# Feed-forward's first product by Strassen's seven sub-products, with nine hidden tiles kept in DRAM

## The reference

```python
def dwconv(x, w):   # three taps along the rows, per column
...
def conv_ffn(h, p):
    u = dwconv(h @ p['w_up'], p['ffn_conv']) + p['ffn_conv_b']
    val, gate = jnp.split(u, 2, axis=-1)
    return (val * jax.nn.silu(gate)) @ p['w_down']
...
        x = x + gt1 * rmsnorm(y, p['g_post_mix'])
        h = modulate(rmsnorm(x, p['g_pre_ffn']), sh2, sc2)
        x = x + gt2 * rmsnorm(conv_ffn(h, p), p['g_post_ffn'])
```

## Time and profile before

| | us |
|---|---|
| three runs: lowest, median, highest | 3891.1, 3891.55, 3891.93 |
| the profiled execution, its own time | 3886.74 |
| its span, first to last instruction | 3885.0 |
| PE busy in the span | 3590.0 (92%) |
| DVE busy, ACT busy | 1754.6 (45%), 962.5 (25%) |
| mean granted TensorE clock | 0.962 of full |

### The profile page before, as it was taken

How to read it: one execution, slowest core, us unless ns; L and a number is a source line. 1 busy time by engine, 2 the same in 40 slices (tenths; PEclk the granted TensorE clock), 3 DMA queues, 4 the chain that set the end, 5 groups by cost and what they waited for, 6 DMA issues and landing times.

```text
span 3885.0 us, 63673 instructions
## 1 busy us (share of the span) xinstructions
PE 3590.0 (92%) x28989; PEld 2243.8 (58%) x28989; DVE 1754.6 (45%) x2533; ACT 962.5 (25%) x1900; POOL 47.3 (1%) x114
## 2 busy tenths in 40 slices
PE   7998879989999996789999998999899799999988
PEld 3546655559988986344444443444566444777753
DVE  2048852245556555332222220022999663544524
ACT  3015620135455553121111110000011301233320
POOL 2000000000000000000000000000000000000000
PEclk9999989989999998899999999999999899999999
...
GB/s 221 22 43 66 66 65 7 28 6 17 4 17 4 4 4 5 114 103 36 30 44 44 43 22 38 44 54 103 22 33 33 43 60 67 22 27 28 1 76 65
DMA packets 108143, 168.08 MB, mean 43 GB/s; under 512 B 5203, under 2 KB 66386, under 8 KB 107234
## 3 DMA queue, kind: packets, MB, share of 16 engines
...
## 4 chain that ended last, share of the span: by engine, by line
PE 84%; DVE 9%; ACT 4%; DMA 2%; issue 1%; SPq 0%; ACTq 0%; DVEq 0%
PE psum_all L66 83%; ACT sbuf_all L75 3%; DVE sbuf_all L102 3%; DVE sbuf_all L94 3%; DVE sbuf_all L84 2%; PE psum_all L69 1%; ACT L75 1%; DMA sbuf_all<-in_w_mod 1%; DMA sbuf_all<-in_w_out 1%; DVE sbuf_all L91 0%; DVE sbuf_all L108 0%; DMA sbuf_all<-in_gla_w_out 0%; DVE sbuf_all L90 0%; DMA sbuf_all<-in_w_up 0%; DMA sbuf_all<-in_w_down 0%
## 5 line engine op out<-in xcount | busy, mean ns | idle before, releaser
...
L75 ACT ACTIVATE sbuf_all<-psum_all 128x512 f32<-128x512 f32 (+7 forms) x969 | 434.6, 468 | 1569.0 <-PE psum_all L66 1441.7
L94 DVE SCALAR_TENSOR_TENSOR sbuf_all<-sbuf_all 128x1040 f32<-128x1040 f32 (+8 forms) x571 | 624.0, 1094 | 24.8 <-PE psum_all L66 4.5
L75 ACT ACTIVATE sbuf_all<-sbuf_all 128x64 f32<-128x64 f32 (+12 forms) x449 | 259.9, 589 | 952.8 <-DVE sbuf_all L78 394.8
L84 DVE TENSOR_TENSOR sbuf_all<-sbuf_all 128x640 f32<-128x640 f32 (+10 forms) x497 | 403.9, 833 | 187.0 <-ACT sbuf_all L75 147.7
L78 DVE COPY sbuf_all<-psum_all 128x256 f32<-128x256 f32 (+5 forms) x137 | 71.1, 526 | 540.5 <-PE psum_all L66 526.4
L91 DVE TENSOR_SCALAR sbuf_all<-sbuf_all 128x1024 f32<-128x1024 f32 (+9 forms) x131 | 76.5, 589 | 470.3 <-ACT sbuf_all L75 467.7
L75 ACT ACTIVATE sbuf_all<-psum_all,sbuf_all 128x1280 f32<-128x1280 f32 (+5 forms) x212 | 164.3, 781 | 351.4 <-PE psum_all L66 323.2
L108 DVE COPY_PREDICATED sbuf_all<-sbuf_all,psum_all 128x256 f32<-128x256 int32 (+2 forms) x296 | 145.5, 493 | 159.3 <-PE psum_all L66 154.5
L69 PE MATMUL psum_all<-sbuf_all 128*128 128x128 f32 (+2 forms) x771 | 115.0, 294 | 56.2 <-DVE sbuf_all L90 27.0
L90 DVE TENSOR_SCALAR sbuf_all<-sbuf_all 128x256 f32<-128x256 f32 (+9 forms) x149 | 57.5, 424 | 209.1 <-ACT sbuf_all L75 206.3
L69 PEld LDWEIGHTS psum_all<-sbuf_all 128*128 128x128 f32 (+2 forms) x771 | 92.9, 152 | 91.8 <-DVE sbuf_all L90 30.1
...
...
## 6 DMA issues: line engine op xcount, KB each, us to landing
sbuf_all<-in_w_mod SPq DMA_DIRECT2D x12, 2048.0 KB, 8.2
...
sbuf_all<-in_w_in SPq DMA_DIRECT2D x6, 2048.0 KB, 7.8
...
sbuf_all<-in_w_down SPq DMA_DIRECT2D x4, 2048.0 KB, 7.6
...
sbuf_all<-in_x ACTq DMA_DIRECT2D x2, 2048.0 KB, 19.9
```

The source lines that it names most:

```text
L75: return self.e.activation(out, in_, func, bias=bias, scale=scale, **kw)
L84: return self.e.tensor_tensor(out, a, b, op) if self.e is not None else Unissued()
L94: return self.e.scalar_tensor_tensor(out, a, s, b, op0, op1) if self.e is not None else Unissued()
```

## The change

`up` takes `h` and each pair of weight tiles as 2 x 2 blocks: the 1024 columns of `h` in two halves of four tiles ("low", "high"), the 1024 rows in two halves of 512, and a value tile and a gate tile as the two outputs. One level of Strassen's scheme (in Winograd's form) makes the four output blocks of a pair from seven products of half the depth, in place of eight. So a pair is 7 x 4 = 28 matmuls where it was 32. The operands are sums and differences: of `h`'s blocks, made once for the stage by VectorE (`row_sums`, four operations of 128x2048, three into new places, one over `rows12`), and of the weights' blocks, made for each pair (`weight_sums`, four operations of 128x512, one of them over the block `w21` in its slot). The outputs are put together from four banks a to d: banks a, c and d take two products each, the second added to the first, with a copy of a (by ScalarE) or an addition out of c or d (by VectorE) between the two. There are five such additions of 128x512 on VectorE per pair, and two bank copies on ScalarE in place of four. The convolution and the multiplication of pair p come while TensorE works on pair p + 1.

The row sums and weight sums lie where the first nine hidden tiles were. Those nine tiles are made in a staging buffer, go out to DRAM on ScalarE's queue (512 KB each), and come back in two loads (one tile, then eight) on SyncE's queue when all engines have ended `up`. `down` takes its weight blocks in another order and size: hidden tiles 15 to 21, then 8 to 14, then 0 to 7. The diff, with the removed bodies of functions that stand above left out:

```diff
-UPS = [(blk, half, gate) for blk in range(KF // 2) for half in range(2) for gate in range(2)]
+UPS = [(blk, half) for blk in range(KF // 2) for half in range(2)]
+SPILLED = 9
 def up_memory(K):
     sb = K.sb
     sb.at = K.hT_at
     K.hid = sb.take(KF * L2, k=KF)
     assert sb.at <= K.h2T_at
     sb.at = K.h2T_at + KD * SEQ
-    K.up_raws = K.slots([sb.take(SEQ + 2) for _ in range(2)])
+    K.up_raws = [sb.take(SEQ + 2) for _ in range(2)]
     K.cv, K.cg = sb.take(SEQ), sb.take(SEQ)
+    K.up_part, K.hid_stage = sb.take(512), sb.take(SEQ)
+    low, high, one, two = slice(0, 4), slice(4, 8), slice(0, 512), slice(512, SEQ)
+    K.rows11, K.rows12, K.rows21, K.rows22 = (K.h2T[:, k, t] for k in (low, high) for t in (one, two))
+    at = K.hT_at
+    K.rows_t1, K.rows_t2, K.rows_t4 = (sb.view(at + i * 2048, 2048, k=4) for i in range(3))
+    K.w_sums = [[sb.view(at + 6144 + 1536 * i + 512 * n, 512, k=4) for n in range(3)] for i in range(2)]
+    assert 6144 + 2 * 1536 <= SPILLED * L2
+    K.hid_dram = K.nc.dram_tensor("hid_spill", (P, SPILLED, SEQ), F32).ap()
+def up_weights(w, half):
+    value, gate = slice(P * half, P * half + P), slice(256 + P * half, 256 + P * half + P)
+    return w[:, 0:4, value], w[:, 4:8, value], w[:, 0:4, gate], w[:, 4:8, gate]
 def up_tensor(K, te):
     U = K.up
     for s in K.mix.ends():
         te.wait_ge(*s)
...
+    def part(bank, lhs, rhs, opens):
+        for k in range(4):
+            done = te.matmul(bank, lhs[:, k, :], rhs[:, k, :], start=opens and k == 0, stop=k == 3)
+        return done
+    for p, (blk, half) in enumerate(UPS):
+        if half == 0:
             w = open_block(K, te, ("up", blk), 512)
...
+        w11, w12, w21, w22 = up_weights(w, half)
+        s1, s2, s4 = K.w_sums[p % 2]
+        a, b, c, d = (open_bank(K, te, "up", p, x) for x in "abcd")
+        part(a, w11, K.rows11, True).then_inc(*U.t.tick("first", p))
+        te.wait_ge(*U.v.by("s2", p))
+        te.wait_ge(*U.v.by("t2"))
+        part(b, s2, K.rows_t2, True).then_inc(*U.t.tick("both", p))
+        te.wait_ge(*U.v.by("s3", p))
+        te.wait_ge(*U.v.by("t3"))
+        part(c, w21, K.rows12, True).then_inc(*U.t.tick("differences", p))
+        part(d, s1, K.rows_t1, True).then_inc(*U.t.tick("sums", p))
+        te.wait_ge(*U.s.by("first", p))
+        part(a, w12, K.rows21, False).then_inc(*U.t.tick("one_one", p))
+        te.wait_ge(*U.v.by("t4"))
+        te.wait_ge(*U.v.by("u3", p))
+        part(c, w22, K.rows_t4, False).then_inc(*U.t.tick("two_one", p))
+        te.wait_ge(*U.v.by("s4", p))
+        te.wait_ge(*U.v.by("two_two", p))
+        part(d, s4, K.rows22, False).then_inc(*U.t.tick("one_two", p))
+        if half:
             K.weights.end(("up", blk), U.t.now())
...
     for s in K.mix.ends():
         se.wait_ge(*s)
     se.wait_ge(*U.g.by("pads"))
...
+    value = K.up_raws[0]
+    def gate(p):
+        se.wait_ge(*U.v.by("conv", p, 1))
+        se.activation(K.cg, K.cg, ACT.Silu).then_inc(*U.s.tick("silu", p))
+    def spill(p):
+        if p < SPILLED:
+            se.wait_ge(*U.v.by("hid", p))
+            se.dma_start(K.hid_dram[:, p, :], K.hid_stage).then_inc(*K.dma("spill_hid").tick(p))
+    for p in range(len(UPS)):
+        se.wait_ge(*U.t.by("first", p))
+        if p:
+            se.wait_ge(*U.v.by("one_two", p - 1))
+        se.activation(K.up_part, K.bank.view("up", p, "a"), ACT.Copy).then_inc(*U.s.tick("first", p))
+        if p:
+            gate(p - 1)
+        se.wait_ge(*U.t.by("one_one", p))
+        if p:
+            se.wait_ge(*U.v.by("conv", p - 1, 0))
+        se.activation(value[:, 1:513], K.bank.view("up", p, "a"), ACT.Copy).then_inc(*U.s.tick("one_one", p))
+        K.bank.end(("up", p, "a"), U.s.now())
+        if p:
+            spill(p - 1)
+    gate(len(UPS) - 1)
 def up_vector(K, ve):
     U = K.up
...
+    T, V, S = U.t, U.v, U.s
     for s in K.mix.ends():
         ve.wait_ge(*s)
...
+    value, gate = K.up_raws
+    part = K.up_part
+    def weight_sums(p):
+        blk, half = UPS[p]
+        w = open_block(K, ve, ("up", blk), 512)
+        w11, w12, w21, w22 = up_weights(w, half)
+        s1, s2, s4 = K.w_sums[p % 2]
+        if p >= 2:
+            ve.wait_ge(*T.by("one_two", p - 2))
+        ve.tt(s1, w21, w22, ALU.add).then_inc(*V.tick("s1", p))
         ve.wait_ge(*V.now())
...
+        ve.tt(s2, s1, w11, ALU.subtract).then_inc(*V.tick("s2", p))
+        ve.tt(w21, w11, w21, ALU.subtract).then_inc(*V.tick("s3", p))
+        ve.wait_ge(*V.by("s2", p))
+        ve.tt(s4, w12, s2, ALU.subtract).then_inc(*V.tick("s4", p))
+    def row_sums():
+        ve.tt(K.rows_t1, K.rows12, K.rows11, ALU.subtract).then_inc(*V.tick("t1"))
+        ve.wait_ge(*V.now())
+        ve.tt(K.rows_t2, K.rows22, K.rows_t1, ALU.subtract).then_inc(*V.tick("t2"))
+        ve.tt(K.rows12, K.rows22, K.rows12, ALU.subtract).then_inc(*V.tick("t3"))
+        ve.wait_ge(*V.by("t2"))
+        ve.tt(K.rows_t4, K.rows21, K.rows_t2, ALU.subtract).then_inc(*V.tick("t4"))
+    def conv(p, half):
+        tile = p + half * KF
+        raw, out = K.up_raws[half], (K.cv, K.cg)[half]
+        taps = [K.col[f"fconv{t}"][:, tile:tile + 1] for t in range(3)]
+        ve.wait_ge(*S.by("one_one", p))
+        ve.wait_ge(*V.now())
+        ve.ts(out, raw[:, 1:1 + SEQ], taps[1], ALU.mult, K.col["ffn_conv_b"][:, tile:tile + 1], ALU.add).then_inc(*V.tick())
         ve.wait_ge(*V.now())
         ve.stt(out, raw[:, 0:SEQ], taps[0], out, ALU.mult, ALU.add).then_inc(*V.tick())
         ve.wait_ge(*V.now())
...
+        ve.stt(out, raw[:, 2:2 + SEQ], taps[2], out, ALU.mult, ALU.add).then_inc(*V.tick("conv", p, half))
+    def hidden(p):
+        ve.wait_ge(*S.by("silu", p))
+        ve.wait_ge(*V.by("conv", p, 0))
+        if 0 < p < SPILLED:
+            ve.wait_ge(*K.dma("spill_hid").by(p - 1))
+        out = K.hid_stage if p < SPILLED else K.hid[:, p, META:L2]
+        ve.tt(out, K.cv, K.cg, ALU.mult).then_inc(*V.tick("hid", p))
+    ve.wait_ge(*U.g.by("pads"))
+    weight_sums(0)
+    row_sums()
+    for p in range(len(UPS)):
+        a, b, c, d = (K.bank.view("up", p, x) for x in "abcd")
+        if p:
+            conv(p - 1, 1)
+            conv(p - 1, 0)
+        ve.wait_ge(*S.by("first", p))
+        ve.wait_ge(*T.by("both", p))
+        ve.tt(part, part, b, ALU.add).then_inc(*V.tick("u2", p))
+        K.bank.end(("up", p, "b"), V.now())
+        if p:
+            hidden(p - 1)
+        ve.wait_ge(*T.by("differences", p))
+        ve.wait_ge(*V.now())
+        ve.tt(gate[:, 513:1025], part, c, ALU.add).then_inc(*V.tick("u3", p))
+        if p + 1 < len(UPS):
+            weight_sums(p + 1)
+        ve.wait_ge(*T.by("sums", p))
+        ve.wait_ge(*V.by("u3", p))
+        ve.tt(gate[:, 513:1025], gate[:, 513:1025], d, ALU.add).then_inc(*V.tick("two_two", p))
+        ve.wait_ge(*T.by("two_one", p))
+        ve.tt(gate[:, 1:513], part, c, ALU.add).then_inc(*V.tick("two_one", p))
+        K.bank.end(("up", p, "c"), V.now())
+        ve.wait_ge(*T.by("one_two", p))
+        ve.tt(value[:, 513:1025], part, d, ALU.add).then_inc(*V.tick("one_two", p))
+        K.bank.end(("up", p, "d"), V.now())
+    last = len(UPS) - 1
+    conv(last, 1)
+    conv(last, 0)
+    hidden(last)
...
-DOWN_K = [(k0, min(KD, KF - k0)) for k0 in range(0, KF, KD)]
+DOWN_K = [(15, 7), (8, 7), (0, 8)]
 def down_memory(K):
...
     banks = [open_bank(K, te, "down", i, 0) for i in range(NT)]
     for k0, kn in DOWN_K:
         w = open_block(K, te, ("down", 0, k0), 512, kn)
+        if k0 < SPILLED:
+            te.wait_ge(*K.dma(f"reload_hid{k0}").final())
         for i in range(NT):
             for k in range(kn):
-                done = te.matmul(banks[i], K.hid[:, k0 + k, META + i * P:META + (i + 1) * P], w[:, k, :], k0 + k == 0,
-                                 k0 + k == KF - 1)
+                done = te.matmul(banks[i], K.hid[:, k0 + k, META + i * P:META + (i + 1) * P], w[:, k, :],
+                                 (k0, k) == (15, 0), (k0, k) == (0, KD - 1))
             done.then_inc(*W.t.tick("down", i, 0))
         K.weights.end(("down", 0, k0), W.t.now())
...
         bank = open_bank(K, te, "down", i, 1)
         for k0, kn, w in blocks:
             for k in range(kn):
-                done = te.matmul(bank, K.hid[:, k0 + k, META + i * P:META + (i + 1) * P], w[:, k, :], k0 + k == 0,
-                                 k0 + k == KF - 1)
+                done = te.matmul(bank, K.hid[:, k0 + k, META + i * P:META + (i + 1) * P], w[:, k, :],
+                                 (k0, k) == (15, 0), (k0, k) == (0, KD - 1))
         done.then_inc(*W.t.tick("down", i, 1))
         turn(i - 1)
     for k0, _ in DOWN_K:
...
 def down_sync(K, sy):
     W = K.down
     w_down = K.io["w_down"][0]
-    for n in range(2):
-        for k0, kn in DOWN_K:
-            load_block(K, sy, ("down", n, k0), w_down, n * 512, 512, k0, kn)
+    for k0, kn in DOWN_K[:2]:
+        load_block(K, sy, ("down", 0, k0), w_down, 0, 512, k0, kn)
```

(5 more changed lines are left out.)

36 lines of the change are left out of this document (1 added, 35 removed).

## The result

| | before | changed |
|---|---|---|
| runs: lowest, median, highest, us | 3889.72, 3891.32, 3891.93 | 3820.49, 3824.34, 3827.11 |
| the profiled execution, its own time | 3886.74 | 3825.82 |
| its span | 3885.0 | 3824.1 |

The changed kernel takes 0.9828 of the time of the kernel before, 95% interval 0.9811 to 0.9845. The difference of the medians is 67.0 us; 66.1 were forecast. The medians themselves are good to some microseconds only, as the runs of one kernel spread by up to 7 us. A second set of runs gives 3825.9 us, ratio 0.9832 (0.9818 to 0.9845).

The account below looks back on a forecast made before the run. TensorE, busy 92% of the span, was taken to bound the kernel. Terms -75.6 + 4.1 + 2.4 + 2.6 + 0.4 = -66.1 us, from 3891.55 to 3825.5 us; the forecast alone spans 3821 to 3833, the range reaching up to 3848.

Parts of the forecast that it names:

- 88 matmuls less: In `up`, 22 pairs go from 32 to 28 matmuls: 176 instructions of 0.4293 us fewer, -75.6 us.
- wait for the sums: At the start of `up`, after its first product, PE waits for VectorE's s2 and t2: +4.1 us, range 3 to 7.
- clock behind it: After the new gap early in `up`, clock at 0.51 for 4.80 us: +2.4 us, range 0 to 4.6.
- the stage's end: At the end of `up`, VectorE's addition, two convolutions and multiplication take 9.0 us against 6.49: +2.6 us, range 2 to 4.
- the last weight block: In `down`, PE waits for a last block of eight tiles instead of six: +0.4 us, from above 1.5.
- a sign of being wrong: In the `up` loop, a mean PE instruction over 0.43 us would show the forecast wrong.
- The cover: In the pair loop, VectorE has 6 us to spare at u3 and two_two, so PE's waits cost 0.
- The rival of the starved loop: In the pair loop, VectorE's waits and added operations starve PE; at 1 us per pair 22 us, 3847; chance 0.07.
- The trip: Nine spills to DRAM and their reloads, 21 us at the 2 MB reload's price, hide behind PE's 96 us: 0.
- The rival of the clock: In the pair loop, shorter groups bring the clock down, 4.6 us per pair, 101 us in all: 3927; chance 0.02.
- The rival of longer instructions: In `up`, instructions an eighth longer, 0.483 us, leave the stage as long and add 9.5 us of gaps: 3901; chance 0.01.

Follow-up runs that it names:

- the kernel with the eighth product back: Changed kernel with every pair's first product done twice, so 32 matmuls per pair again: 3897.53 us, ratio 1.0015 to the kernel before.
- the filled-gap kernel: Changed kernel with the first product done twice in the first pair only, putting matmuls of no use in the gap at the start of `up`: 3825.3 us.
- the kernel with the early convolution: Changed kernel with the gate's convolution moved ahead of the last addition, in the last pair only: 3824.25 us.

## Why the prediction was right

By its own steps, for the piece, which is 64.8 us shorter:

| step | forecast | measured | from |
|---|---|---|---|
| 88 matmuls less | -75.6 | -74.9 | 604.50 - 3.67 - (527.60 - 1.7) |
| wait for the sums | +4.1 | +3.9 | gap 3.92 |
| clock behind it | +2.4 | +1.7 | 527.60 - 525.90 |
| the stage's end | +2.6 | +2.6 | 10.82 - 8.23 |
| the 352 instructions behind the gap at `down` | not priced | +1.1 | 153.75 - 152.69 |
| the last weight block | +0.4 | +0.7 | 8.41 - 7.70 |
| the 44 instructions behind it | 0 | +0.2 | 20.70 - 20.53 |
| sum | -66.1 | -64.7 | |

- **The instructions** kept their time; the pair's 24.05 us against a forecast of 24.04 shows it, and the kernel with the eighth product back shows that nothing else earned the gain. The mean over the run of 1224, 527.60 / 1224 = 0.431 us, is over the 0.43 that the prediction named as a sign of being wrong, but by the stretch at the lower clock alone, which it had forecast itself: without it the mean is 525.90 / 1224 = 0.4297. Of the 0.7 us short of 75.6, 0.24 are the end of the extra run (8 instructions between gaps take 3.67, not 3.43 us); the rest is too small to place.
- **The cover** of 6 us at u3 was right, and it was tested from both sides: 4.4 us of extra work cost nothing, 8.7 us cost 2.65 us of wait in each pair. The rival of the starved loop falls for this kernel, but its edge is not far: past it a wait of 2.65 us per pair cost 75 us.
- **The wait for the sums** was 3.92 us, near the 4.1 forecast in part because two small errors cancel. VectorE's row is

```profile
1735.13 11.56 DVE L84 TENSOR_TENSOR sbuf_all<-sbuf_all 128x512 f32<-128x512 f32 x8 [0.98 <-POOL sbuf_all L81]
```

  It began 0.29 us behind PE, where the prediction had both start together, and its eight sums (four of them 128x2048, which the row lumps in) took 11.56 us without a break, where the prediction's prices come to 12.2.
- **The clock** behind the new gap was the right mechanism and a little too dear: 2.4 us by the nearest row, the gap of 4.20 us, and 1.7 measured.
- **The clock at `down`** is a term that the sum does not have. The prediction took that gap as 2.6 us longer and let the clock behind it stay as it was; the row of 352 instructions is 1.1 us longer, with the granted clock at 0.77 over its first 10.69 us against 0.87 over 10.83 us before. That the longer gap did this is not shown: with the same gap of 10.82 us the filled-gap kernel has 152.84 us and a clock of 0.86 there, and with a gap of 7.99 us the kernel with the early convolution has 153.45 us. The cause of the 1.1 us stays open.
- **The last weight block** has a gap 0.7 us longer in this trace, against 0.4 forecast from its size. The size is not shown to be the reason: where a block of seven tiles came last (tiles 0 to 7 first) the gap was 8.52 us, no shorter than the 8.41 us with eight.
- **The trip** was rightly set at nothing. Its price was put too high: 21 us by the row of a 2 MB reload, 13.6 by its own.
- **The rival of the clock** in shorter groups: the granted clock is 1.00 over 514 us, although the bank changes every eight instructions. With real gaps of 2.65 us in each pair the clock fell in six of the 21 full pairs. The rule of the Trainium skill (TensorE: Matmul & The Clock Gate, A second HAM failure mode: psum-queue depth-cycling) speaks of small idles between the groups; in this loop PE has none, so the rule had nothing to act on here.
- **The rival of longer instructions** was worked out a little wrong: with 1232 instructions for 1408, a stage as long as before needs each to cost a seventh more (0.491 us), not an eighth (0.483). Nothing in the forecast hangs on it.

The mechanism was right in the steps that carry the sum. That 66.1 and 67.0 lie within 1 us of each other is in part luck: by the piece the forecast is 1.3 us off, the steps' errors of 0.2 to 1.1 us partly cancel, and the medians carry the spread of the other stages. The two profiled executions differ by 60.9 us, mostly since the stages ahead of `up` took 4.9 us more in the second.
